# The first tile of the second block's input projection multiplies un-normalised chunks, and its outputs are scaled and shifted afterwards

## What is computed

```python
def first_block(...):
    ...
        h = modulate(rms_norm(x, ffn2_norm[l]), sh3, sc3)
        x = x + 0.5 * g3[:, None, :] * swiglu(h, ffn2_w_gate[l], ffn2_w_up[l], ffn2_w_down[l])
    return rms_norm(x, final_norm)

def second_block(...):
        h = rms_norm_2(x, g_pre_mix[l]) * (1.0 + sc1[:, None]) + sh1[:, None]
        proj = h @ w_in[l]
        (q_n, kc, vc, ksl, vsl, kw, vw, gl,
         q_d, k_d, v_d, qi, ki, wi) = jnp.split(proj, splits, axis=-1)
        o_nsa = nsa_attention(...)
        o_dsa = dsa_attention(...)      # qi, ki, wi choose the keys (top k)
```

## Time and profile before

| | |
|---|---|
| time, median of 3 runs | 1777.46 us (1776.95 to 1779.31) |
| the profiled execution's own time | 1779.18 us |
| its span, first to last instruction | 1777.4 us |
| busy, share of the span | PE 99%, DVE 57%, ACT 22%, POOL 67% |

### The profile page before, as it was taken

How to read it: one execution, slowest core, us unless ns; L and a number is a source line. 1 busy time by engine, 2 the same in 40 slices (tenths; PEclk the granted TensorE clock), 3 DMA queues, 4 the chain that set the end, 5 groups by cost and what they waited for, 6 DMA issues and landing times.

```text
span 1777.4 us, 24781 instructions
## 1 busy us (share of the span) xinstructions
PE 1755.3 (99%) x8745; PEld 1388.3 (78%) x8745; DVE 1009.3 (57%) x1701; ACT 389.7 (22%) x845; POOL 1186.8 (67%) x1182
## 2 busy tenths in 40 slices
PE   8999999999999999999999999999999999999998
PEld 6888888887876788888888888878446778888887
DVE  4855345576655205785414556898974987007712
ACT  3111000012246212210000001454885110000111
POOL 4676767686665477767676668765754678667763
PEclk9999999999999999999999999998999999999999
DMA  9655465542330132455436533513000322232321
GB/s 356 213 189 180 143 195 187 174 154 66 101 97 26 32 111 87 150 180 187 135 96 203 187 119 95 127 51 95 25 25 1 95 72 95 96 99 92 102 100 56
DMA packets 242478, 212.96 MB, mean 120 GB/s; under 512 B 45985, under 2 KB 236894, under 8 KB 242398
## 3 DMA queue, kind: packets, MB, share of 16 engines
q1 hardware_dynamic: 226368, 211.18, 37.2%
q10 hardware_dynamic: 16030, 0.72, 0.6%
HBM read 209.72 MB, written 2.10 MB: 119 GB/s over the span
## 4 chain that ended last, share of the span: by engine, by line
PE 72%; POOL 12%; issue 8%; DVE 5%; DMA 2%; ACT 1%; ACTq 0%; POOLq 0%; DVEq 0%; SPq 0%
PE ps L792 19%; PE ps L793 18%; PE ps L794 18%; POOL w_lo L721 8%; PE ps L1455 2%; POOL w_hi L716 2%; PE ps L1442 2%; PE ps L1215 2%; PE ps L1475 2%; POOL w_hi L715 2%; DMA raw<-in_ffn_w_down 1%; PE ps L1236 1%; PE ps L1224 1%; PE ps L833 1%; DMA raw<-in_ffn_w_gate 0%
## 5 line engine op out<-in xcount | busy, mean ns | idle before, releaser
L721 POOL TENSOR_TENSOR w_lo<-raw,w_hi 128x512 fp32r<-128x512 f32 (+4 forms) x576 | 740.4, 1315 | 11.8
L792 PE MATMUL ps<-h_hi,w_hi 128*128 128x512 f32 x1240 | 487.5, 393 | 2.2 <-DVE h_lo L2719 1.4
L794 PE MATMUL ps<-h_hi,w_lo 128*128 128x512 f32 x1240 | 483.8, 390 | 0.0
L793 PE MATMUL ps<-h_lo,w_hi 128*128 128x512 f32 x1240 | 483.6, 390 | 0.0
L713 POOL TENSOR_TENSOR w_hi<-raw,ones 128x8 fp32r<-128x8 f32 x144 | 34.6, 240 | 440.7 <-PE ps L794 386.2
L792 PEld LDWEIGHTS ps<-h_hi,w_hi 128*128 128x128 f32 x1240 | 233.1, 188 | 57.7 <-issue 7.5
L794 PEld LDWEIGHTS ps<-h_hi,w_lo 128*128 128x128 f32 x1240 | 233.1, 188 | 49.5
L793 PEld LDWEIGHTS ps<-h_lo,w_hi 128*128 128x128 f32 x1240 | 233.2, 188 | 47.7
L792 PE MATMUL ps<-g_hi,w_hi 128*128 128x512 f32 x608 | 237.8, 391 | 0.1
L794 PE MATMUL ps<-g_hi,w_lo 128*128 128x512 f32 x608 | 236.6, 389 | 0.0
L793 PE MATMUL ps<-g_lo,w_hi 128*128 128x512 f32 x608 | 236.6, 389 | 0.0
(11 more groups left out here) (433 smaller groups left out, 2394.3 us busy)
## 6 DMA issues: line engine op xcount, KB each, us to landing
ada<-in_ada_w SPq DMA_DIRECT2D x31, 1024.0 KB, 7.1
ada<-in_w_ada SPq DMA_DIRECT2D x24, 1024.0 KB, 7.0
raw<-in_ffn_w_gate SPq DMA_DIRECT2D x22, 1024.0 KB, 5.2
raw<-in_ffn_w_up SPq DMA_DIRECT2D x22, 1024.0 KB, 5.2
raw<-in_w_in SPq DMA_DIRECT2D x16, 1024.0 KB, 5.1
raw<-in_w_up SPq DMA_DIRECT2D x16, 1024.0 KB, 5.3
raw<-in_w_down SPq DMA_DIRECT2D x16, 1024.0 KB, 5.0
raw<-in_ffn_w_down SPq DMA_DIRECT2D x16, 768.0 KB, 4.6
```

What stands on the lines that cost most here:

```text
L721: last = pool.tensor_tensor(lo[:, c], src[:, c], hi[:, c].bitcast(F32), ALU.subtract)
L792: pe.matmul(o, wh, xh, start=start, stop=False)
L793: pe.matmul(o, wh, xl, start=False, stop=False)
L794: return pe.matmul(o, wl, xh, start=False, stop=stop)
```

## The change

`W_IN2` is now run by `plain_tile` too, as norm 3 (`N_FINAL_PRE`). ACT makes the high parts of the un-normalised chunks (`plain_high`) beside the squares, DVE the low parts; DVE also makes the shift's product (`shift_sums(3)`) between chunks 5 and 6 of the down product. PE starts the tile before the norm is known and runs the sums at chunk 2, the turn at chunk 3 and the spread at chunk 4. The idle products are gone. The chunks are still normalised by `modulated` for the tiles behind (now written over the un-normalised ones). DVE keeps the inverse, scales both outputs of the tile in PSUM, and ACT adds the shift (`shifted`) ahead of each raw copy.

```diff
@@ PE
-        def group(o, n, kc, cols, c0, m, xh, xl, k0=0, start=True, stop=True, middle=None):
+        def group(o, n, kc, cols, c0, m, xh, xl, k0=0, start=True, stop=True, middle=None, h_ready=None):
             for k in range(kc):
+                if h_ready is not None:
+                    pe.wait_ge(h_hi_done, h_ready + k + 1)
+                    pe.wait_ge(h_lo_done, h_ready + k + 1)
...
                     norm_sum(i)
+                    if i == N_FINAL_PRE:
+                        final_sum()
                 elif k == 3:
                     norm_turn(i)
...
         run_ffn(1)
-        norm_sum(N_FINAL_PRE)
-        final_sum()
-        norm_spread(N_FINAL_PRE)
...
-        signal(pair_of_groups((1, 0), n, 24, rp_mm, high_first=True), rp_mm, 1, 2)
+        plain_tile(N_FINAL_PRE, (1, 0), rp_mm)
         final_spread()
@@ ACT
-                norm_squares(act, 3, x_ready, X_F2B, xT, chunks=range(4))
-                sines(tab2, 1)
-                root_table(act)
-                norm_squares(act, 3, x_ready, X_F2B, xT, chunks=range(4, NC))
+                for m in range(NC):
+                    if m == 4:
+                        sines(tab2, 1)
+                        root_table(act)
+                    norm_squares(act, 3, x_ready, X_F2B, xT, chunks=(m,))
+                    plain_high(act, 3, x_ready, X_F2B, chunks=(m,))
...
+        def shifted(i):
+
+            act.wait_ge(z_scaled, 2 + i + 1)
+            act.activation(ps[:, raw_bank(i)], ps[:, raw_bank(i)], ACT.Identity,
+                           bias=shift_out[N_FINAL_PRE][:, i:i + 1]).then_inc(z_shifted, 1)
+            act.wait_ge(z_shifted, i + 1)
+
         def raw_copy(i):
             wait_rot2(act, i)
+            if i < 2:
+                shifted(i)
@@ DVE
-                    chunks_then_add(3, down)
+                    plain_chunks(3, down)
...
         norm_inverse(N_FINAL_PRE)
-        modulated(3, A_PREMIX, 72)
         dve.wait_ge(f_std, 1)
         dve.reciprocal(rb[:, P:2 * P], std[:, P:2 * P]).then_inc(f_inv, 1)
+        modulated(3, A_PREMIX, 72)
         dve.wait_ge(h_lo_done, 32)
+        keep_inverse(N_FINAL_PRE)
+        for m in range(2):
+            wait_rot2(dve, m)
+            dve.tensor_tensor(ps[:, raw_bank(m)], ps[:, raw_bank(m)], sq_sum2[:], ALU.mult).then_inc(z_scaled, 1)
@@ SP
+            if n == W_IN2 + 2:
+                sp.wait_ge(shift_summed, 3)
```

More of the change, by code:

```diff
@@ L180, in build @@
     gain2, postmix2 = vec[:, 208:216], vec[:, 216:224]
-    shift_out = {1: vec[:, 224:226], 2: vec[:, 226:228]}
-    shift_sum = tt[:, 0, 0:256]
+    shift_out = {1: vec[:, 224:226], 2: vec[:, 226:228], 3: vec[:, 228:230]}
     arena = -(-used[0] // 512) * 512
@@ L259, in build @@
     rp_raw2 = place("rp_raw2", [P, 2, T], at=at(72))
+    shift_index = place("shift_index", [P, 256], at=at(76))
+    shift_sum = {1: tt[:, 0, 0:256], 2: tt[:, 0, 0:256], 3: shift_index}
     kc = place("kc", [P, T + CMP_STRIDE], at=at(76))
@@ L324, in build @@
     z_hi_done, z_lo_done, z_used, z_scaled = (sem(f"plain_{s}") for s in ("high", "low", "used", "scaled"))
+    z_shifted = sem("plain_shifted")
     shift_summed, shift_mm = sem("shift_summed"), sem("shift_mm")
@@ L360, in build @@
     ON_DVE = NC - 2
-    IDLE_NORMS = (N_FINAL_PRE,)
-    PLAIN = {1: (W_MIX, A_MIX, 24, h_hi, h_lo), 2: (W_FFN2, A_FFN2, 48, z_hi2, z_lo2)}
+    PLAIN = {1: (W_MIX, A_MIX, 24, h_hi, h_lo), 2: (W_FFN2, A_FFN2, 48, z_hi2, z_lo2),
+             N_FINAL_PRE: (W_IN2, A_PREMIX, 72, h_hi, h_lo)}
+    B_SHIFT = {1: B_NORM2, 2: B_NORM2, 3: 7}
     def squared(i, m):
@@ L856, in norm_sum @@
             for m in range(ON_DVE, NC):
-                if m == NC - 1 and i in IDLE_NORMS:
-                    idle_products(4, 0)
                 pe.wait_ge(n_sq, squared(i, m))
@@ L880, in norm_spread @@
             else:
-                if i in IDLE_NORMS:
-                    idle_products(2, 0)
                 norm_turn(i)
-                if i in IDLE_NORMS:
-                    idle_products(2, 0)
                 pe.wait_ge(n_inv, i + 1)
                 columns_spread(norm_bank(i)).then_inc(n_rb, 1)
-                if i in IDLE_NORMS:
-                    idle_products(7, 0)
         def final_sum():
@@ L904, in plain_tile @@
             wh, wl = slot(w_hi, n, NC, 256), slot(w_lo, n, NC, 256)
-            pe.wait_ge(x_ready, (X_F1B, X_MIX)[i - 1] + 6)
+            pe.wait_ge(x_ready, (X_F1B, X_MIX, X_F2B)[i - 1] + 6)
             for k in range(NC):
@@ L909, in plain_tile @@
                     for m in range(2):
-                        last = pe.matmul(ps[:, B_NORM2, m:m + 1], shift_sum[:, P * m:P * m + P], ones[:, 0:1],
+                        last = pe.matmul(ps[:, B_SHIFT[i], m:m + 1], shift_sum[i][:, P * m:P * m + P], ones[:, 0:1],
                                          start=True, stop=True)
@@ L929, in plain_tile @@
                         last.then_inc(first_done, 1)
-                if i == 1 and k < NC - 1:
+                if i != 2 and k < NC - 1:
                     last.then_inc(z_used, 1)
@@ L1329, in proj @@
             cols = plan[n][2]
-            last = group(ps[:, raw_bank(r[0])], n, NC, cols, P * half, P, h_hi, h_lo, middle=middle)
+            last = group(ps[:, raw_bank(r[0])], n, NC, cols, P * half, P, h_hi, h_lo, middle=middle,
+                         h_ready=24 if r[0] == 2 else None)
             signal(last, rp_mm, 1 if cols == P else half, 2)
@@ L1652, in plain_high, with wait_plain_used @@
             act.activation(zh[:, m], xT[:, m], ACT.Identity, scale=fac[:, factor + m:factor + m + 1]).then_inc(z_hi_done, 1)
-    def wait_plain_used(eng, m):
-        eng.wait_ge(z_used, m + 1) if m < NC - 1 else eng.wait_ge(tile_used, W_MIX + 1)
+    def wait_plain_used(eng, i, m):
+        eng.wait_ge(z_used, (i // 2) * (NC - 1) + m + 1) if m < NC - 1 else eng.wait_ge(tile_used, PLAIN[i][0] + 1)
     def mod_high(act, i, shift, chunks=range(NC)):
@@ L1660, in mod_high @@
             act.wait_ge(h_t, 8 * i + m + 1)
-            if i == 1:
-                wait_plain_used(act, m)
+            if i in (1, N_FINAL_PRE):
+                wait_plain_used(act, i, m)
             act.activation(h_hi[:, m], scaled(i, m), ACT.Identity, bias=mod[:, shift + m:shift + m + 1]).then_inc(h_hi_done, 1)
@@ L2113, in shift_sums @@
             w = raw[:, n % 2].rearrange("p (k c) -> p k c", c=256)
-            step(dve.tensor_scalar(shift_sum, w[:, 0], column(mod, shift), None, ALU.mult))
+            sums = shift_sum[i][:, 0:256]
+            step(dve.tensor_scalar(sums, w[:, 0], column(mod, shift), None, ALU.mult))
             for k in range(1, NC):
-                ins = dve.scalar_tensor_tensor(shift_sum, w[:, k], column(mod, shift + k), shift_sum, ALU.mult, ALU.add)
+                ins = dve.scalar_tensor_tensor(sums, w[:, k], column(mod, shift + k), sums, ALU.mult, ALU.add)
                 if k < NC - 1:
@@ L2121, in keep_inverse @@
         def keep_inverse(i):
-            step(dve.tensor_copy(sq_sum[:], norm_of(i)))
+            step(dve.tensor_copy((sq_sum2 if i == N_FINAL_PRE else sq_sum)[:], norm_of(i)))
         def plain_chunks(i, chunk):
@@ L2136, in plain_chunks @@
             dve.wait_ge(shift_mm, i)
-            step(dve.tensor_copy(shift_out[i], ps[:, B_NORM2, 0:2]))
+            step(dve.tensor_copy(shift_out[i], ps[:, B_SHIFT[i], 0:2]))
         def modulated(i, factor, shift, chunks=range(NC)):
@@ L2150, in modulated @@
                     dve.wait_ge(h_t, 8 * i + k + 1)
-                    if i == 1:
-                        wait_plain_used(dve, k)
+                    if i in (1, N_FINAL_PRE):
+                        wait_plain_used(dve, i, k)
                     dve.scalar_tensor_tensor(h_lo[:, k], scaled(i, k), column(mod, shift + k), h_hi[:, k].bitcast(F32),
```

## The result

The changed kernel takes 1793.28 us (median of 5 runs, 1792.12 to 1794.88), the kernel before 1777.46 us beside it: the ratio is 1.0085, 95% interval 1.0074 to 1.0096. That is slower by some 15 us. The forecast was 1791.8 us with a range from 1785 to 1797. The profiled execution after has a span of 1793.1 us; before it was 1777.4, so the two traces differ by 15.7 us.

What follows compares the result with a forecast made beforehand. Two chains, PE's and DVE's, arriving together were taken to bound the kernel. +8.5, +1.5, +1.6 and -0.6 gave +11.0 us; +3.3 for the clock made +14.3 on the median 1777.46: 1791.8 us, range 1785 to 1797.

Steps and rivals of the forecast that it cites:

- last square later: Down product: DVE's added low parts and shift sums make ACT's last square end at about 1120.6 instead of 1112.15, +8.5 us.
- norm's chain, without clock: From last square to `modulated`: chunks 2 and 3 now stand in it, 5.0 us instead of 3.45, +1.5 us.
- clock at the first waits: PE waits about 6 us before the last square; half clock behind it loses 1.4 us (bounds 0 and 2.5).
- scale and shift, to `natural(0)`: Behind `modulated`: DVE's scaling and ACT's shifts precede the inverse's copy, so `natural(0)` starts 11.6 us later; +1.6 us.
- clock at `natural(0)`: PE waits about 8 us before `natural(0)`; half clock there loses 1.9 us (bounds 0 and 2.5).
- given back behind: Behind `natural(0)`, PE's 0.6 us of idle time absorbs that much of the delay, -0.6 us.
- DVE in the down product: Five low parts (5.0 us) and shift sums (8.7) against 6.3 us of DVE waits; chunk 7's add 7.4 us later.
- PE can start at 1110.7 and reaches the sums at 1113.5: Tile start on PE: chunks 0 and 1 begin at 1110.7, 1.50 us each with turn, sums at about 1113.5.
- The sentence that the late square covers this: POOL's own split of the tile may slow under DVE's work, but PE's wait for the last square covers it.
- rival 1: Clock stays at 2.4 GHz through both PE waits, or its loss is given back: +11.0, 1788.5 us; chance 0.27.
- Rival 2: Down product: shift sums at their fastest, 3.9 us, low parts at 0.75, POOL's split finished first: +5.0, 1782.5 us; chance 0.10.
- Rival 3 and 4: 3: PE's stretch shrinks to sums, turn, spread, -3.9 us, 1773.6, chance 0.05. 4: delay made up behind 1135, no change, 0.03.

Runs made afterwards that it cites:

- the one with both fillers: Changed kernel plus products nobody reads in two PE waits: 14 ahead of the norms' sums, 32 ahead of the wait for the copied inverse; 1788.33 us, ratio 1.0051.
- the copy first: Changed kernel with ACT copying the final norm's inverse ahead of the two raw copies, not behind them; 1790.74 us, ratio 1.0066.
- the kernel with scale and shift: Changed kernel without seven of eight shift sums, with unread products ahead of the tile's split (8) and the inverse's copy (32); 1784.81 us, ratio 1.0039.
- the one without them: Changed kernel without seven shift sums, with unread products in two PE waits, also without DVE's inverse copy and scalings and ACT's two shifts; 1784.87 us, ratio 1.0040.

## Why the prediction was right

Term by term, from the two traces and the one with both fillers:

| term | predicted | measured |
|---|---|---|
| last square later | +8.5 | +8.46 |
| norm's chain, without clock | +1.5 | +1.7 (5.17 - 3.45) |
| clock at the first waits | +1.4 | +2.7 (7.87 - 5.17) |
| scale and shift, to `natural(0)` | +1.6 | +1.8 (21.28 - 19.44) |
| clock at `natural(0)` | +1.9 | +2.0 (18.31 - 16.35) |
| given back behind | -0.6 | -1.4 (0.55 to the second index scores, 0.89 from there to `ex_hi`) |
| sum | +14.3 | +15.2 |

The offset of 0.89 us adds to it, 0.4 us come back behind `ex_hi`, and the traces end 15.7 us apart. The chain is the forecast one, term for term. That the sum is off by only 0.9 us is in part luck: the first fall of the clock cost 1.3 us more than forecast, and 0.8 us more came back behind.

- *DVE in the down product*: five low parts, 0.74 + 1.36 + 1.20 + 1.35 + 0.74 = 5.4 us (5.0 forecast), sums 9.3 (8.7), the wait for ACT behind its sines 2.17 (2.0). The waits of 6.3 us that were to absorb it are all gone. Each piece was a little larger than forecast, by 1.1 us in all, and DVE's other work a little shorter (the angle tables before chunk 6 took 3.87 us instead of 4.90), so that the term came out so close is in part luck.
- *PE can start at 1110.7 and reaches the sums at 1113.5* was wrong: the split of the tile ended at 1113.60 (1111.18 before), PE started at 1113.70 and reached the sums at 1117.0. PE's wait for the last two squares was therefore 2.79 + 0.90 us and not about 6. The sentence that the late square covers this held, so it cost nothing in the changed kernel; without the sums it is what PE waits for.
- *The clock*: it fell at both places, so rival 1 is out. The term of the first fall was mis-sized: I took the 1.4 us of the shorter row, and it cost 2.7: the half clock fell on the serial part for which DVE waits, the last sums, chunk 2, the turn and half of chunk 3. In the trace with the copy first the same fall cost 1.5, so the price has a spread that one row can't give. The rule of the Trainium skill ("TensorE: Matmul & The Clock Gate", "HAM oscillation — how this bites in real kernels") gave the direction rightly: 0.50 behind both waits.
- *Rival 2*, sums at their fastest: its price for the sums was right (0.34 + 3.61 us with POOL at rest, 3.9 forecast), its condition, a split that has ended by then, was met in no run; holding POOL back gained nothing. Cheap sums without that condition would not have given its +5.0 either: without the sums and with the clock at 1.00, `modulated` is still 6.8 us late, behind the split of the tile, where rival 2 has 2.5 + 1.5 = 4.0.
- *Rival 3 and 4*: PE met the late square and the late copy, and behind 1135 only 1.4 us came back.

## What to carry to other kernels

Before a multiplication is moved across a matmul to free one engine's waiting time, count what the engine that now does the extra work has idle in that stage: here 6.3 us of DVE's waits against 14.7 us of low parts and sums. Count what runs beside it as well: DVE's sums and POOL's split ran beside each other here, and whichever was put first, PE waited for the other. Ask too when the weights are ready that the earlier start needs: here their split set a start from which the norm came late even without the sums. And where PE's filler work is removed with the stretch it filled, price the low clock as a range, at the matmuls behind the new wait for which another engine waits: in these traces 1.5 to 2.7 us at the first place and 1.3 to 2.6 at the second.

## What the runs showed of the hardware

- A 128x256 product with both inputs in SBUF took 0.52 us (3.61 / 7) with POOL at rest and 1.27 us (8.92 / 7) beside POOL's split, and POOL's four 128x512 subtractions took 5.60 us beside the sums, 5.04 in the trace before, and 6.13 without the sums, beside DVE's angle tables, adds and low parts. The Trainium skill ("SBUF — State Buffer", "Who interferes with whom") says that a DVE instruction with two SBUF inputs contends with a GpSimd instruction that reads SBUF, and that the lock is exclusive; the rows agree in direction. In the chain that ended last the sums in the middle, beside the subtractions of 1.40 us each (5.60 / 4), follow each other at 1.43 us, close to POOL's pace:

```profile
1108.26 1.41 DVE shift_index L2127
1109.69 1.41 DVE shift_index L2127
1111.12 1.41 DVE shift_index L2127
```

- A wait of 2.02 us left the granted clock at 1.00 in one kernel (low parts cut), one of 2.26 us was followed by 0.50 in another (sums left out), and in the kernel before without idle products one of 1.66 us, with two short ones of 0.93 and 0.27 ahead of it, by 0.63 and 0.52. So the length of the wait alone doesn't decide, and no run here shows what does.
- A later stretch of narrow matmuls takes more or less by where the clock falls in it. The same 64 matmuls in the chain that ended last, in the kernel before and in the one without idle products:

```profile
1224.93 5.92 PE ps L1429 x64
```

```profile
1225.27 3.69 PE ps L1429 x64
```

Neither kernel holds the change, and they differ by 2.2 us here: from 1226 to 1228 the clock is at 0.51 in the one and at 1.00 in the other. All fourteen traces fall into two groups by it. Where the 64 matmuls take 3.69 to 4.21 us, it is 584.8 to 585.4 us from the start of `ex_hi` to the end of the span; where they take 4.61 to 5.92, it is 586.7 to 587.3. The kernel before and the changed one are both in the second group; the one with the copy first, the one without the sums and the one with both fillers are in the first, so 1.5 to 2 us of what their spans gain is made here and not by their edits. This is why an earlier `ex_hi` doesn't always show in the time: the kernel with scale and shift is in the first group (3.69 us), the one without them in the second (4.97), and behind `ex_hi` it loses 1.8 us, all of the 1.7. This holds for the profiled executions; the runs without a profile don't show it.
